# A hybrid delta-rule and latent-attention step on one core: the last delta chunk runs into the output branches, attended products lie two heads behind, and three starts are re-ordered

## What is computed

```python
h = _rms(x, p['norm_gain']) * (1 + scale) + shift
(qkv_raw, z_a, beta_raw, alpha_raw, q_raw, ckv_raw, kr_raw, z_b, g_a, g_b) = _split_in(h @ p['w_in'])
o_a, conv_new, s_new = _deltanet(qkv_raw, beta_raw, alpha_raw, conv_buf, s0, p)
o_b, ckv_new, kr_new = _mla(q_raw, ckv_raw, kr_raw, pos, past_ckv, past_kr, p)
u_a = o_a * jax.nn.silu(z_a)
u_b = o_b * jax.nn.silu(z_b)
merged = jax.nn.sigmoid(g_a) * (u_a @ p['w_o_dn']) + jax.nn.sigmoid(g_b) * (u_b @ p['w_o_mla'])
y = x + gate * (merged @ p['w_out'])
```

## Time and profile before

| | us |
|---|---|
| median of 3 runs (lowest to highest) | 2096.97 (2096.0 to 2098.93) |
| profiled execution | 2098.45 |
| its span, first to last instruction | 2096.8 |
| PE busy in the span | 1963.6 (94%) |
| mean granted clock of TensorE | 0.973 of full speed |

### The profile page before, as it was taken

The page is one execution under the profiler, slowest core; times in us unless marked ns, Lnnn a source line. Parts: engine busy times, 40 slices in busy tenths (PEclk is TensorE's granted clock), DMA queues, the critical chain, the costliest instruction groups (busy, mean ns, idle before and its releaser), DMA issues.

```text
span 2096.8 us, 31960 instructions
## 1 busy us (share of the span) xinstructions
PE 1963.6 (94%) x12287; PEld 1804.8 (86%) x12287; DVE 858.0 (41%) x1858; ACT 683.8 (33%) x1493; POOL 200.0 (10%) x258
## 2 busy tenths in 40 slices
PE   6899999999999999989995788997999997999999
PEld 2699999999999999987774667776999996999877
DVE  1545554300010000106644555555667776433333
ACT  2333333311121122213332344335576774121110
POOL 0012121001000000000002221111101010000000
PEclk9899999999999999999997999999999998999999
DMA  9322222333222222121102221115123225533321
GB/s 328 103 97 88 113 85 96 116 135 107 85 96 105 96 85 96 71 67 52 46 18 71 71 62 46 37 37 155 42 62 101 82 62 162 195 103 113 100 81 65
DMA packets 154028, 195.61 MB, mean 93 GB/s; under 512 B 9457, under 2 KB 125214, under 8 KB 153932
## 3 DMA queue, kind: packets, MB, share of 16 engines
q1 hardware_dynamic: 142444, 151.85, 21.5%
q0 software_dynamic: 10224, 38.13, 5.5%
q10 hardware_dynamic: 1264, 4.39, 0.5%
HBM read 134.15 MB, written 60.19 MB: 93 GB/s over the span
## 4 chain that ended last, share of the span: by engine, by line
PE 84%; DVE 5%; issue 4%; ACT 3%; DMA 2%; DVEq 1%; POOLq 0%; SPq 0%; ACTq 0%; POOL 0%
PE PS L2209 41%; PE PS L1487 10%; PE PS L1320 9%; PE PS L390 6%; PE PS L1419 5%; PE PS L1492 3%; PE PS L731 2%; PE PS L706 2%; PE PS L2225 2%; PE PS L719 1%; DMA Wraw<-in_w_ada 1%; PE PS L692 1%; DVE amx L951 1%; ACT E L1664 1%; PE PS L306 1%
## 5 line engine op out<-in xcount | busy, mean ns | idle before, releaser
L2209 PE MATMUL PS<-HH,WL 128*128 128x352 f32 (+1 forms) x1752 | 380.0, 325 | 5.2 <-DVE mod L2319 5.2
L2209 PE MATMUL PS<-HH,WH 128*128 128x352 f32 (+1 forms) x1752 | 378.4, 323 | 0.0
L2209 PE MATMUL PS<-HL,WH 128*128 128x352 f32 (+1 forms) x1752 | 378.0, 324 | 0.0
L2209 PEld LDWEIGHTS PS<-HH,WL 128*128 128x128 f32 (+1 forms) x1752 | 298.9, 189 | 5.6 <-issue 5.3
L2209 PEld LDWEIGHTS PS<-HH,WH 128*128 128x128 f32 (+1 forms) x1752 | 301.1, 188 | 0.3
L2209 PEld LDWEIGHTS PS<-HL,WH 128*128 128x128 f32 (+1 forms) x1752 | 297.8, 188 | 0.2
L2315 DVE TENSOR_TENSOR WL<-Wraw,WH 128x2048 fp32r<-128x2048 f32 x37 | 84.8, 2293 | 516.2 <-ACT WH L2149 516.2
L2177 ACT ACTIVATE R<-PS 128x1056 f32<-128x1056 f32 x48 | 50.5, 1053 | 405.5 <-PE PS L2209 405.5
L807 ACT ACTIVATE pr<-PS,amx,qsc 128x128 f32<-128x128 f32 (+8 forms) x72 | 58.0, 805 | 169.5 <-DVE amx L953 169.5
L1487 PE MATMUL PS<-WT,QL 128*128 128x128 f32 x832 | 102.4, 276 | 1.1 <-DVE QL L1877 0.9
L731 PE MATMUL PS<-V,pT 128*128 128x128 f32 (+1 forms) x624 | 87.7, 285 | 16.0 <-ACT pT L823 15.9
(11 more groups left out here) (300 smaller groups left out, 3090.1 us busy)
## 6 DMA issues: line engine op xcount, KB each, us to landing
scratch_proj<-R SPq DMA_DIRECT2D x72, 576.0 KB, 2.8
Wraw<-in_w_in POOLq DMA_DIRECT2D x30, 1024.0 KB, 5.4
QKV<-scratch_proj SPq DMA_DIRECT2D x27, 512.0 KB, 5.1
Wraw<-in_w_ada SPq DMA_DIRECT2D x12, 1024.0 KB, 5.6
fr<-scratch_u SPq DMA_DIRECT2D x16, 528.0 KB, 7.0
gr<-scratch_proj SPq DMA_DIRECT2D x16, 528.0 KB, 3.6
qT<-scratch_proj SPq DMA_DIRECT2D x9, 512.0 KB, 5.2
zb<-scratch_proj SPq DMA_DIRECT2D x18, 256.0 KB, 3.2
```

The source lines that it names most:

```text
L2209: last = pe.matmul(PS[0:m, psum + b, 0:TB], w[:, s, k, c * P:c * P + m], h[:, k, b * TB:(b + 1) * TB], start=(k == 0 and first), stop=(k = ...
```

## The change

**Start of attention.** `load_q` has two slots, and the loads of query tiles 0 and 1 are both issued in the latents stage. In the last key tile the three "q" turns of tile 0 move ahead of the second half of the value products, ACT's reads of them ahead of its copy of the values, and 18 `pe_busy` products stand behind the last turned keys.

**Attention.** Values are multiplied two heads behind the scores instead of one (`pT` has three slots), narrow tiles turn their probabilities in banks 4 and 5 by turns, the three "q" turns stand one head apart, "o" jobs come two heads later, the normalisation of a group and the norms of the next tile one head later.

**Start of delta.** The scaled copies of the first keys leave `act_k` and come behind the squares of the queries; POOL's masks wait for the first norms; the first product of keys and queries moves behind the first level's turn; six `pe_busy` become three; the identities of levels 2 to 6 are placed one level at a time.

**Delta's end and branches.** The fourth `meet` is gone. ACT and DVE split the first weights and the eight rows of u between the steps of the delta tail, one norm chain serves the last two chunks, the last two turns of outputs lie inside and behind branch chunk 1, SP loads rows 4 to 7 and the first gate rows inside the delta stage. A chunk uses banks n%2, n%2+2, n%2+4, and a merge is three instructions instead of one.

```diff
     def sp_latents(sp):
...
         load_q(sp, 0)
+        load_q(sp, 1)
...
+                if half == 0 and isinstance(t, int) and t == NKT - 1:
+                    for part in range(3):
+                        pe_job(pe, ("q", 0, part))
...
+            pe_keys_back(pe, t)
             if isinstance(t, int) and t == NKT - 1:
-                for part in range(3):
-                    pe_job(pe, ("q", 0, part))
-            pe_keys_back(pe, t)
+                pe_busy(pe, 18, 1)
...
-            (0, EARLY): [("q", 1, 0)]}
+            (0, LATE): [("q", 1, 0)]}
     for i in range(NQ):
         for g in range(2):
-            jobs.setdefault((H * i + 4 * g + 5, EARLY), []).append(("o", 2 * i + g, 0))
-        for step, phase, kind, part in ((-1, EARLY, "q", 0), (-1, LATE, "q", 1), (0, LATE, "q", 2), (6, EARLY, "b", 0), (6, LATE, "b", 1)):
+            jobs.setdefault((H * i + (7, 11)[g], EARLY), []).append(("o", 2 * i + g, 0))
+        for step, phase, kind, part in ((-1, LATE, "q", 0), (0, LATE, "q", 1), (1, LATE, "q", 2), (6, EARLY, "b", 0), (6, LATE, "b", 1)):
...
         pe.wait_ge(s_ex, x + 1)
-        if x:
+        if narrow(x) and narrow(x - 1) and narrow(x - 2):
+            pe.wait_ge(s_pa, x - 1)
+        elif x:
             pe.wait_ge(s_pa, x)
...
-            if 1 <= x <= NX:
-                pe_values(pe, x - 1)
+            if 2 <= x <= NX + 1:
+                pe_values(pe, x - 2)
             if x < NX:
                 pe_transposes(pe, x)
...
-            if 1 <= x % H <= 3 and x // H + 1 < NQ:
-                dve_q_norms(dve, x // H + 1, x % H - 1)
+            first = 2 if x >= H else 1
+            if first <= x % H <= first + 2 and x // H + 1 < NQ:
+                dve_q_norms(dve, x // H + 1, x % H - first)
...
+    def dve_merge(dve, n):
...
+        for b in range(NB):
+            cols = slice(b * TB, (b + 1) * TB)
+            last = dve.tensor_tensor(out[:, cols], PS[:, n % 2 + 2 * b, 0:TB], gr[:, n % 2, cols], ALU.mult)
...
     def pe_branches(pe):
...
             if n == 0:
-                pe_busy(pe, 3, 7)
+                for g in range(2):
+                    pe.wait_ge(d_u, nth(NT - 2, g))
+                    pe.wait_ge(d_o1, nth(NT, g))
+            if n == 1:
+                for g in range(2):
+                    pe.wait_ge(d_s, nth(NT, g))
+                    pe.wait_ge(d_o2, nth(NT, g))
...
-            if n == 0:
-                pe_busy(pe, 4, 7)
             for k in range(KD):
+                if n == 1 and k == 5:
+                    for g in range(2):
+                        pe_out(pe, NT - 1, g, psum=PS[:, 6 + g])
...
+            if n == 1:
+                for g in range(2):
+                    pe.wait_ge(d_u, nth(NT - 1, g))
+                    pe_out(pe, NT, g, psum=PS[:, 6 + g])
...
     def sp_delta(sp):
...
         sp_load_za(sp, NT)
-        sp_store_u(sp, NT - 1)
+        for r in range(NFR, KD):
+            sp.wait_ge(s_fl, r - NFR + 1)
+            sp_u_row(sp, r)
+        for g in range(2):
+            sp.wait_ge(d_st, nth(NT, g))
+        for n in range(2):
+            sp_gate_rows(sp, n)
+        sp_w_o(sp, 2)
...
-        pe_busy(pe, 6, 6)
-        for g in range(2):
-            pe_qk(pe, 0, g)
         for g in range(2):
             pe.wait_ge(d_qq, nth(0, g))
+        pe_busy(pe, 3, 4)
...
+                if n == 0 and l == 0:
+                    for g in range(2):
+                        pe_qk(pe, 0, g)
...
     def act_delta(act):
...
+        act_w_o_hi(act, 0)
+        for r in range(KD):
+            act_u_row_hi(act, r)
+        act.wait_ge(s_nrm, NT + 3)
         for g in range(2):
             act_squares(act, NT, g)
-        for g in range(2):
-            act_normalise(act, NT, g)
+        act.wait_ge(s_nrm, NT + 4)
+        for t in (NT - 1, NT):
+            for g in range(2):
+                act_normalise(act, t, g)
...
+        act_w_o_hi(act, 1)
...
         pool.memset(S[:, 0], 0.0).then_inc(s_clear, 1)
+        pool.wait_ge(s_nrm, 1)
...
+        dve_w_o_lo(dve, 0)
+        for r in range(KD):
+            dve_u_row_lo(dve, r)
         for g in range(2):
             dve_output(dve, NT, g, b=3)
         for g in range(2):
             dve_state(dve, NT, g)
...
+        dve_merge(dve, 0)
+        for g in range(2):
+            dve_u(dve, NT - 1, g, psum=PS[:, 6 + g])
...
+        dve_w_o_lo(dve, 1)
+        for g in range(2):
+            dve_u(dve, NT, g, psum=PS[:, 6 + g])
```

More of the change, by code:

```diff
@@ L622, in build, with narrow, turned_bank @@
         second.append(second[-1] + (len(keys_of(x // H)[2]) > 4))
+    def narrow(x):
+        return x >= 0 and len(keys_of(x // H)[2]) <= 4
+    def turned_bank(x):
+        return 4 + (x % 2 if narrow(x) else 0)
     def scores_of(x):
@@ L639, in sp_attention @@
                 sp.dma_start(scr["gcum"].rearrange("t h n -> (t h) n"), gcT).then_inc(s_so, 16)
-            if i + 1 < NQ:
-                sp.wait_ge(s_t7, turn[("q", i, 0)] + 1)
+            if 1 <= i and i + 1 < NQ:
+                sp.wait_ge(s_t7, turn[("q", i - 1, 0)] + 1)
                 if i >= 2:
@@ L741, in pe_attention @@
         pe_scores(pe, 0)
-        for x in range(NX + 2):
+        for x in range(NX + 4):
             if x + 1 < NX:
@@ L1017, in build @@
     QKV = sb(p3, "QKV", [P, 3, 3 * H, P])
+    E = per_group("E")
+    Em = per_group("Em")
+    Es = per_group("Es")
+    NL = per_group("NL")
+    QL = per_group("QL", NL7)
+    WT = per_group("WT")
+    sq = per_group("sq")
+    sb(p3, "delta_spacer_1", [P, 872])
+    XT = per_group("XT")
+    RR = per_group("RR")
+    Z = per_group("Z")
+    O1 = per_group("O1")
+    O2 = per_group("O2", 2)
+    ON = per_group("ON")
+    UA = per_group("UA", 2)
     RS = sb(p3, "RS", [P, 3, 16])
@@ L1183, in gates @@
             sp_gate_rows(sp, n)
-        for r in range(NFR, KD):
-            row(r)
-            if r == NFR:
-                for n in range(2):
-                    sp_gate_rows(sp, n)
-        weights(2)
         for r in range(KD, KD + NFR):
@@ L1287, in dve_branches @@
+    def dve_branches(dve):
+        dve_gate_diagonal(dve)
+        dve.drain()
+        for n in range(1, KD - 1):
+            if n == 3:
+                dve.wait_ge(s_so, 48)
+            dve_merge(dve, n)
+            if n == 2:
+                dve_gate(dve)
+            if n % 2:
+                dve_w_o_lo(dve, n // 2 + 2)
+        for r in range(KD, 2 * KD):
             if r == 2 * KD - 1:
-                merge(KD - 1)
-            dve.wait_ge(s_fh, r + 1)
-            dve.tensor_tensor(FL[:, r % KD], fr[:, r % NFR], FH[:, r % KD].bitcast(F32), ALU.subtract).then_inc(s_fl, 1)
+                dve_merge(dve, KD - 1)
+            dve_u_row_lo(dve, r)
```

229 lines of the change are left out of this document (108 added, 121 removed).

## The result

The changed kernel takes 2075.06 us (median of 4 runs, 2073.9 to 2077.78) beside 2097.18 us for the kernel before: the ratio is 0.9896 (95% interval 0.9881 to 0.9911), a gain of 19 to 25 us. The forecast was 2060, its range 2047 to 2071. The sign is right, the size is not.

The account below looks back on a forecast made before the run. PE was taken as the bound, with 84% of the chain of waits. Terms -1.1 - 20.5 - 4 - 13 + 0.15 = -38.5 us took the profiled 2098.45 to 2060; range 2047 to 2071, the forecast's own 2052 to 2068.

Parts of the forecast that it names:

- Start of attention: Up to the first scores: load's wait exchanged for the fills, gain only from full clock; -1.1 us (-4 to +2).
- Attention: Attention tiles: removed waits for copy, squares and "o" job give -20.5 us, of which -11.4 in tiles 0 to 3.
- The floors: Tiles 0 to 3: least times by DVE 17.6, 18.9, 20.2, 21.2 us; by PE 13.7, 19.1, 20.4, 25.7.
- a sign of being wrong: Attention tiles 0 to 3: turns wait for the exponential as long as the values did for the copy.
- Rival B: Narrow attention tiles: waits only change their name, tiles 0 to 3 give 4 us; -30 in all, 2068 us; chance 0.20.
- The wide tiles: Attention's wide tiles: PE stays the bound, -8.5 us counted from removed waits, -1 lost to jobs in new places.
- Start of delta: Delta's start to second level's turn: norms begin 2 us earlier, ready 6 earlier, masks behind them; -4 us (-1.5 to -6).
- Delta's end: Delta's end to branch chunk 2: splits and rows overlap the delta tail, chunk 2 starts earlier; -13 us (-9 to -16).
- Rival F: Delta's end: chunk 1 waits for the last state behind eight rows on DVE; gain 5, not 13; 2068 us; chance 0.06.
- One sign: Delta's end: branch chunk 0 was to end before DVE's last output.
- C: All covers hold: narrow tiles near their floors (-18 us), attention's start -4; -47 in all, 2051 us; chance 0.13.
- D: Tiles 0 to 3 at half clock throughout: +34 us in place of -11, 2105 us in all; chance 0.04.

## Why the prediction was wrong, point by point

**Start of attention: the number right by luck.** Meeting at 1125 and first score at 1133 were forecast; they came at 1125.1 and 1133.1. But of the 1.05 us gained, all was there at the end of the projections (936.93 instead of 937.99), which the change does not touch, so the term itself is nothing: what the turns and fills gained at full clock (1.07 instead of 1.94, 3.60 instead of 4.49) went into the later meeting. "The load's wait is exchanged for the fills, almost one for one" is right, and the runs with fewer fills put the price at 8.8.

**Attention: the step that failed.** It is the sentence that sets the four tiles at 18.5, 22, 24 and 28. The prediction took the row "values wait for ACT's copy" as a wait that a lag removes. But the copy was late because the next head's exponential stood ahead of it in ACT's queue, and that because DVE's maximum stood behind norms; the turn before it was done in time. The next turn needs the same exponential, so the lag took PE past the wait for the copy and into the wait for that. (No run put the copy ahead of the exponential in ACT's queue.) The floors were made from DVE's busy time spread evenly over a tile; DVE's work lies in a pile in heads 2 to 5, and there it is the bound. The turn's wait for the exponential, 13.2 us where the values had waited 14.7, is what the prediction itself named as a sign of being wrong. Rival B, at 2068, had this mechanism and was given 0.20; even that counted 4 us in these tiles, where 1 came. Two more parts went missing: the clock, which fell in tile 2 (1.00 to 0.81), so that PE's own work in the four tiles grew from 78.8 to 81.6, and SP's queue, where an "o" job two heads later put the loads later. That queue was named for delta's end, and overlooked here. The wide tiles gave 5.4 of the 8.5 counted (164.53 to 159.08 in tiles 4 to 7). One reading was wrong as well: not all of POOL's 6.8 us follow on the norms, only its last three steps do, some 3 us; the rotation before them waits for ACT alone.

**Start of delta: near in sum, partly by luck, wrong in one part.** Norms began 2.2 earlier after delta's start (forecast 2) and were ready 6.1 earlier (forecast 6). But the masks behind the norms earned nothing, as the run with the masks beside them shows; the prediction counted them in. The changed kernel's 20.2 us hold a stretch at half clock (its products of keys and queries took 3.29, 1.95 where the clock held), without which the term would be -5. So a part that gave nothing and a stretch at half clock that was not forecast stand on either side of a sum that looks right. What is left for the gain are the scaled copies, the moved product and fewer fills; they were not taken apart.

On the ports, the strict matrix took 1.13 for four steps while POOL's third mask ran (1436.86 to 1438.12), and again 1.13 for four with POOL done (the rows above). The Trainium skill ("SBUF — State Buffer", Who interferes with whom) states that a DVE step with at most one SBUF input, outside its two-port modes, does not contend with GpSimd, and that one with two contends with a GpSimd step that reads SBUF. The trace agrees with the first half, and the steps with two inputs, stretched to 1.08 to 1.18, agree with the second. The fourth stretched step (L1865, 1.15) has one tensor input; whether it ran in a mode that the rule excepts, no run shows.

**Delta's end: right.** -13.8 measured, -13 forecast. The whole lay 10.3 earlier by then (delta's last product), and za was asked 10.5 earlier with it, so the prediction's times can be held against these less 10.3: the last FL at 1766.3 (forecast 1777), chunk 1 at 1769.8 (1780.5), chunk 2 at 1786.0 (1797), all within 1 us. The fifth row waited 3.10 for its load (3.60 before), chunk 1 stood 1.24 for the last state, chunk 2 2.58 for the second weights:

```profile
1760.00 1.09 ACT L1243 ACTIVATE FH<-fr 128x1056 fp32r<-128x1056 f32 x1 [3.10 <-DMA fr<-scratch_u]
```

```profile
1769.76 0.72 PE L1342 MATMUL PS<-FH,VL 128*128 128x352 f32 x3 [1.24 <-DVE S L1900]
...
1785.97 1.25 PE L1342 MATMUL PS<-FH,VL 128*128 128x352 f32 x3 [2.58 <-DVE VL L1271]
```

Rival F, chunk 1 held by the state, exists and costs 1.2 us, not 8. One sign did not come: chunk 0 ended at 1768.5, behind DVE's last output (1767.5) and not ahead of it. No run took this part apart; it rests on the two traces.

**Rivals C and D** did not come. Half clock in tiles 0 to 2 grew from 24 to 37 us, far from the 85 that D needed.

## What to carry to other kernels

A wait names the last link, not the cause: before a lag or another buffer is priced, follow the chain of the releaser back to the engine whose queue holds it up, and lay that engine's queue out head by head rather than as busy time over a tile. Where a job moves later, list what stands behind it in every queue that carries its consequences, the DMA queue's too. Fills ahead of a meeting are free only up to the time at which the others arrive. An engine that issues loads ahead of a meeting comes to it only when the last is issued.

## What the runs showed of the hardware

At attention's end a store of 256 KB landed 2.2 us after its issue where no load was in flight (before, the first and the last of three). It took 4.7 us in the changed kernel and 7.2 us in the run with finer norms (medians of two), where loads moved some 345 GB/s around it. The Trainium skill ("DMA: Bandwidth & Descriptors", Latency and other measured facts) says that a DMA's fixed cost is smaller under lighter load of the memory; the rows agree in direction. They do not measure that cost, since the longer times also hold the sharing of the DMA engines with the loads. And what PE did ahead of the second meeting left no mark behind the first score: attention tile 0 took 20.42, 20.42 and 20.43 us with 18, 6 and 1 fills.
